# In-projection, retention, combination and RG-LRU of a hybrid decoder step run as one stage

## The reference, cut to what matters

```python
h = rmsnorm(x, norm_mix)                   # 1024 + 64 tokens, 1024 features
q, k, v, g, xl, yl = split(h @ w_in)       # 256, 256, 512, 512, 512, 512 columns
# retention, 4 heads, chunks of 128 tokens (samples: one chunk of 8 with their own state)
att = (q_c @ k_c.T) * decay
o   = att @ v_c + (q_c * q_dec) @ S
S   = S * c_dec + (k_c * k_dec).T @ v_c
ret = head_rms(o, ret_g) * silu(g)
# RG-LRU
x = causal_conv(xl)                        # 4 taps
r, i = sigmoid(x @ w_rg + b), sigmoid(x @ w_ig + b)   # 4 diagonal blocks of 128
a = exp(-8 r softplus(-lam));  b = sqrt(1 - a^2) * i * x
hl = scan(h_t = a_t h_{t-1} + b_t)
out = concat(ret, hl * gelu(yl)) @ w_out   # then residual, FFN, and layer 1
```

## Time and profile before

| | us |
|---|---|
| median of 3 runs | 3221.49 (3220.18 to 3224.18) |
| the profiled execution, its own time | 3216.29 |
| its span in the trace | 3214.6 |
| granted TensorE clock, mean | 0.95 |
| TensorE matmul / weight load busy | 2972.2 / 2810.3 |
| VectorE / ScalarE / GpSimd busy | 1359.8 / 757.0 / 183.7 |
| chain that ended last | TensorE 39%, DMA 2%, VectorE 2%, ScalarE 1% of the span |

### The profile page before, as it was taken

One profiled execution on the slowest core, in us unless ns is written; L12 is line 12 of the kernel. 1 busy time (PEld: TensorE's weight loads), 2 busy tenths in 40 slices (PEclk: granted clock), 3 DMA queues, 4 the chain that ended last, 5 costly groups with the idle time before them and its releaser, 6 DMA issues. The chain is left out here.

```text
span 3214.6 us, 47394 instructions
## 1 busy us (share of the span) xinstructions
PE 2972.2 (92%) x21277; PEld 2810.3 (87%) x21277; DVE 1359.8 (42%) x1651; ACT 757.0 (24%) x1082; POOL 183.7 (6%) x298
## 2 busy tenths in 40 slices
PE   6997852999999999999999799898899999999997
PEld 6997641999999999999999576666799999999997
DVE  4121248254343444445551255555543444443443
ACT  3100136131111111113221444444421111111110
POOL 0101110000000000002001111111000000000000
PEclk8998556999999999999999899999999999999999
DMA  5323110211111111112223766765301111111111
GB/s 180 110 82 122 51 56 21 84 40 53 40 40 40 53 40 42 51 53 97 82 82 96 271 212 198 249 206 172 134 28 48 45 40 53 50 43 40 40 40 56
DMA packets 130406, 276.23 MB, mean 86 GB/s; under 512 B 8737, under 2 KB 86773, under 8 KB 129696
## 3 DMA queue, kind: packets, MB, share of 16 engines
q1 hardware_dynamic: 107648, 184.83, 17.8%
q0 software_dynamic: 19136, 82.83, 7.5%
q10 hardware_dynamic: 3424, 5.57, 0.5%
HBM read 233.88 MB, written 39.33 MB: 85 GB/s over the span
## 5 line engine op out<-in xcount | busy, mean ns | idle before, releaser
L229 PE MATMUL psum<-h_hi,w_hi 128*128 128x364 f32 x2688 | 594.2, 330 | 18.2 <-DVE h_lo L355 7.2
L229 PE MATMUL psum<-h_hi,w_lo 128*128 128x364 f32 x2688 | 595.5, 330 | 0.0
L229 PE MATMUL psum<-h_lo,w_hi 128*128 128x364 f32 x2688 | 595.3, 329 | 0.0
L229 PEld LDWEIGHTS psum<-h_hi,w_hi 128*128 128x128 f32 x2688 | 468.1, 189 | 18.9 <-issue 13.3
L229 PEld LDWEIGHTS psum<-h_hi,w_lo 128*128 128x128 f32 x2688 | 469.2, 189 | 0.0
L229 PEld LDWEIGHTS psum<-h_lo,w_hi 128*128 128x128 f32 x2688 | 468.0, 189 | 0.0
L213 ACT ACTIVATE w_hi<-w_raw 128x2048 fp32r<-128x2048 f32 x96 | 183.7, 1914 | 830.8 <-PE psum L229 784.1
L1327 DVE TENSOR_TENSOR x_res<-x_res,psum 128x1092 f32<-128x1092 f32 x176 | 227.3, 1291 | 207.6 <-PE psum L229 207.6
L452 PE MATMUL psum<-w_hi,h_lo 128*128 128x256 f32 x992 | 278.7, 281 | 0.0
L452 PE MATMUL psum<-w_hi,h_hi 128*128 128x256 f32 x992 | 278.0, 280 | 0.0
L452 PE MATMUL psum<-w_lo,h_hi 128*128 128x256 f32 x992 | 277.9, 280 | 0.0
(11 more groups left out here) (313 smaller groups left out, 3169.2 us busy)
## 6 DMA issues: line engine op xcount, KB each, us to landing
cache_tile<-in_cache_k SPq DMA_DIRECT2D x64, 512.0 KB, 9.2
cache_tile<-in_cache_v SPq DMA_DIRECT2D x64, 512.0 KB, 3.7
w_raw<-in_w_ffn_gate SPq DMA_DIRECT2D x22, 1024.0 KB, 5.2
w_raw<-in_w_ffn_up SPq DMA_DIRECT2D x22, 1024.0 KB, 5.1
w_raw<-in_w_ffn_down SPq DMA_DIRECT2D x22, 1024.0 KB, 4.8
w_raw<-in_w_in_att SPq DMA_DIRECT2D x12, 1024.0 KB, 7.1
w_raw<-in_w_in_rec SPq DMA_DIRECT2D x10, 1024.0 KB, 5.2
park_x<-x_res POOLq DMA_DIRECT2D x2, 4368.0 KB, 15.4
```

The lines of the kernel that those rows point to most:

```text
L229: mm = pe.matmul(PS[:, bank + c, 0:CW], st[:, slot, wc:wc + P], mv[:, k, c * CW:(c + 1) * CW], start=(i < NCH), stop=(i >= 3 * NCH * nk - ...
```

## The change

Stages 2 to 5 and the output projection's stage become one. Nothing of the projections goes to DRAM any more, and the kernel has 4 meetings where it had 8.

- Stage 1: VectorE copies all 9 turned tiles. ScalarE squares x in its token-major form with a running sum as it arrives; the chain of 1/rms and the diagonal tile are made there, so the feature-major squares, their sums and the sums' matmuls of the first norm are gone. `split_lo(0)` and the vectors come in the middle.
- Order of the blocks: `COL = (6, 8, 7, 9, 0, 1, 2, 3, 4, 5)`, that is x, y, x, y, q, k as 12 feature-major tiles, then v and gate, 18 token-major units each. Tiles 0, 1, 4, 5 are x of the groups 0 to 3, tiles 2, 3, 6, 7 are y.
- RG-LRU: VectorE and ScalarE follow `D_ORDER` and `A_ORDER`, into which the tile evacuations ("ev"), the splits ("w") and the groups' steps are written. `GR`, `GI`, `AA`, `SA` and `YB` are single buffers. The gate matmuls of group j stand inside feature-major tile 2j+2 as three pairs, before the slices k = 2, 4 and 6, in banks 6 and 7; pair c waits until ScalarE has read pair c-1.
- Retention: q and k stay in SBUF; `first(c)` (turned keys, q times k) and `second(c)` (output, state) stand between the v units, `second(t-2)` after the even and `first(t-1)` after the odd unit of token tile t. The output is token-major (attention as the stationary operand), and the head norm is done on it at once by a small chain (`squares`, `inverse`, `root`, `scale`).
- Gate: 18 token-major units with silu in token-major form, each result turned by two transposes (`turn`) two units later and placed by ScalarE (`place`). The samples' retention lies between these units.
- Output projection: `high`/`low` split its operands as soon as the last gate unit has used the slices (`KO` order, LRU's first); its first tile follows slice by slice.
- Pool: X is parked after four small loads; the retention tables are loaded after the last LRU group; X comes back after the last turn.

The diff, cut to its core:

```diff
+        for f in range(2 * N_FM):
+            if f % 2 == 0:
+                pe.wait_ge(wl_done, f // 2 + 1)
+            if f >= 2:
+                pe.wait_ge(fm_out, f - 1)
+            fm_tile(pe, 3 * (f % 2), f // 2 % RING, col_tiles(f % 2), hook(f), HHI, HLO, fm_in)
...
+                if f in YF[0:1] + XF[2:3] + YF[2:3] + (8,) and k in (2, 4, 6):
+                    gates(f // 2 - 1, k // 2 - 1)
...
+        def gates(j, c):
+            if c == 0:
+                pe.wait_ge(l_d, dn["c2", j])
...
+            if 3 * j + c:
+                pe.wait_ge(g_out, 2 * (3 * j + c))
+            for bank, wt in ((6, WR), (7, WI)):
+                pe.matmul(PS[:, bank, 0:CW], wt[:, j, :], XC[j % 2][:, c * CW:(c + 1) * CW],
+                          start=True, stop=True).then_inc(g_in, 1)
...
+    D_ORDER += conv(0) + conv(1) + [("w", 3), ("ev", YF[0])] + scan(0) + [("gi", 0), ("g", 0), ("m", 0)]
+    D_ORDER += [("ev", YF[1]), ("gi", 1), ("g", 1), ("w", 4)] + conv(2) + scan(1) + [("m", 1)]
+    D_ORDER += conv(3) + [("w", 5), ("ev", YF[2]), ("gi", 2), ("g", 2)] + scan(2) + [("m", 2)]
+    D_ORDER += [("ev", YF[3]), ("gi", 3), ("g", 3), ("w", 6), ("ev", 8)] + scan(3) + [("m", 3)]
+    D_ORDER += [("ev", 9), ("w", 7), ("ro", 0), ("ev", 10), ("ev", 11), ("w", 8)]
+    A_ORDER = [("x", 0), ("x", 1), ("w", 3)] + [(x, 0) for x in ("ri", "e", "t", "a", "sq", "q", "gt")]
+    A_ORDER += [("q", 1), ("w", 4), ("gt", 1), ("ri", 1), ("e", 1), ("t", 1), ("x", 2), ("a", 1), ("sq", 1)]
+    A_ORDER += [("x", 3), ("w", 5)] + [(x, 2) for x in ("ri", "e", "t", "q", "gt", "a", "sq")]
+    A_ORDER += [("q", 3), ("w", 6), ("gt", 3)] + [(x, 3) for x in ("ri", "e", "t", "a", "sq")] + [("w", 7), ("w", 8)]
...
+            elif x == "ri":
+                act.wait_ge(l_sp, 6)
+                if j:
+                    act.wait_ge(l_d, dn["m", j - 1])
+                for c in range(NCH):
...
+        pe.wait_ge(l_out, 1)
+        for t in range(NT):
...
+            unit(2 * t, 6, t)
+            if t >= 2:
+                second(t - 2)
...
+            unit(2 * t + 1, 7, t)
+            if t >= 1:
+                first(t - 1)
...
+        for u, (b, t) in enumerate(GSEQ):
...
+            unit(2 * NT + u, 8 + b, t)
+            if u == 0:
+                second(NCHK - 1)
+                sample_first()
+            if u == 2:
+                sample_out()
+            if u == 3:
+                sample_state(0)
+            if u == 4:
+                sample_turn()
+            if u == 5:
+                sample_state(1)
+            if u >= 2:
+                turn(u - 2)
```

More of the change, by code:

```diff
@@ new lines, in prep_sums, with prep_spread @@
+    def prep_sums(pe, q):
+        prep_wait(pe, q, "sq_sum", KT - 1)
+        for t in range(NT):
+            mm = pe.matmul(PS[:, 7, 2 * t:2 * t + 2], sq_buffer(q, 0)[0][:, win(t):win(t) + P], ones[:, 0:2],
+                           start=True, stop=True)
+        mm.then_inc(prep_sem["sums"], 1)
+    def prep_spread(pe, q, parts):
+        prep_wait(pe, q, "diag", 1)
+        for bank, t0, m in parts:
+            if t0 == KT:
+                prep_wait(pe, q, "spread_out", 1)
+            for t in range(t0, t0 + m):
+                r0 = t * P - win(t)
+                mm = pe.matmul(PS[:, bank, (t - t0) * P:(t - t0 + 1) * P - r0], ones[:, :], DIA[:, t, r0:P],
+                               start=True, stop=True)
+            mm.then_inc(prep_sem["spread"], 1)
@@ L408, in prep_spread @@
[L408 to L434 removed]
+            if t == 5:
+                split_lo(dve, 0, 0)
+                dve.wait_ge(vt_done, 1)
+                dve.tensor_copy(vec[:, :], PS[:, 7, 0:NV])
@@ L570, in build, with tm_unit @@
+            if used is not None and i < KT - 1:
+                mm.then_inc(used, 1)
+        return mm
+    def tm_unit(pe, bank, slot, t, done, cols=None):
+        return tm_part(pe, bank, slot, t, range(KT), None, None, cols).then_inc(done, 1)
     stages = {e: [] for e in ("pe", "act", "dve", "pool")}
@@ L995, in s5_act, with tok_scale, rec_act @@
+    v3 = lambda t: t.rearrange("p (c w) -> p c w", c=NCH)
+    def tok_scale(t, half):
+        if t < QT:
+            return RHF[:, t:t + 1] if half else rtok[:, t, 0:1]
+        return RSM[:, 1:2] if half else RSM[:, 0:1]
+    def rec_act(act):
+        for k in range(KT):
+            prep_hi(act, q2, G_MIX[0], k)
+        spread_out(act, q2, SPREAD[:2])
+        split_hi(act, 1, 1, first=True)
+        spread_out(act, q2, SPREAD[2:])
+        split_hi(act, 2, 2, first=True)
         act.activation(SC[:, 0, :], vec[:, V_LAM:V_LAM + 4], ACT.Abs).then_inc(l_sp, 1)
@@ new lines, in rec_act @@
+        for u in range(NGU):
+            if u == NGU - 1:
+                high(0)
+            gate(u)
+            if u == 0:
+                squares(NCHK - 1)
+                act.wait_ge(s_kt, 1)
+                act.wait_ge(r_s, NCHK)
+                act.activation(KTS[:, :, :].rearrange("p h k -> p (h k)"), PS[0:NS, 0, 0:RH * DK],
+                               ACT.Copy).then_inc(s_kts, 1)
+                split_hi(act, 10, 10 % RING)
+            if u == 1:
+                root(NCHK - 1)
+            if u == 2:
+                act.wait_ge(s_o, 1)
+                for e in range(2):
+                    op = act.activation(OS[:, :, :].rearrange("p (g e) w -> p e g w", e=2)[:, e],
+                                        PS[:, (3, 0)[e], 0:2 * NS].rearrange("p (g w) -> p g w", g=2), ACT.Copy)
+                op.then_inc(s_os, 1)
+            if u == 4:
+                squares(QT)
+            if u == 5:
+                root(QT)
+            if u >= 2:
+                place(u - 2)
@@ L1047, in s5_dve, with rec_dve @@
+        for i in range(1, 4):
+            high(i)
+        place(NGU - 2)
+        place(NGU - 1)
+        for i in range(4, KT):
+            high(i)
+        split_hi(act, 11, 11 % RING)
+        split_hi(act, 12, 12 % RING)
+        act.wait_ge(s_ss, 64)
+    def rec_dve(dve):
+        for k in range(KT):
+            prep_low(dve, q2, G_MIX[0], k)
+        split_lo(dve, 1, 1)
+        split_lo(dve, 2, 2)
         dve.wait_ge(l_sp, 3)
@@ new lines, in rec_dve, with gate @@
+        dve.wait_ge(fm_out, 2 * N_FM)
+        for t in range(NT):
+            if t >= 2:
+                state(t - 2)
+                inverse(t - 2)
+            if t >= 1:
+                decay(t - 1)
+            if t >= 2:
+                scale(t - 2)
+            if t >= 1:
+                attend(t - 1)
+        split_lo(dve, 9, 9 % RING)
+        def gate(u):
+            b, t = GSEQ[u]
+            n = P if t < QT else NS
+            dve.wait_ge(tm_out, 2 * NT + u + 1)
+            dve.scalar_tensor_tensor(GG[u % 2][0:n, :], GT[u % 2][0:n, :], 1.0, GG[u % 2][0:n, :], ALU.add,
+                                     ALU.mult).then_inc(m_u, 1)
+            dve.wait_ge(m_u, u + 1)
+            dve.wait_ge(r_oo, t + 1)
+            dve.scalar_tensor_tensor(GT[u % 2][0:n, :], GG[u % 2][0:n, :], 0.5, ON[0:n, t, b * BW:(b + 1) * BW], ALU.mult,
+                                     ALU.mult).then_inc(m_in, 1)
@@ L1651, in cache_load @@
             if j == 0:
[L1652 removed]
+                sp.wait_ge(met, 4 * 2)
             if u == 8:
```

1339 lines of the change are left out of this document (670 added, 669 removed).

## The result

| | before | after |
|---|---|---|
| median, us | 3220.84 (3219.20 to 3224.18) | 3050.22 (3048.41 to 3056.48) |
| ratio | | 0.9472, 95% interval 0.9456 to 0.9489 |
| the profiled execution, its own time | 3216.29 | 3056.48 |
| its span | 3214.6 | 3054.7 |
| mean granted clock | 0.95 | 0.98 |

What follows compares the result with a forecast made beforehand. Bound before the output projection by a chain over VectorE, ScalarE, DMA and slow TensorE, behind it by TensorE's queue. Steps put the second evacuation at 417.7 against 593.4, -175.7: 3040.6 profiled, plus 5.2 gives median 3046; range 3018 to 3085.

Steps and rivals of the forecast that it cites:

- (a): Stage 1: VectorE copies nine tiles and makes the norm's chain and diagonal; +2.5 us, first matmul at 31.7.
- (b): Twelve feature-major tiles with gate matmuls: 24.7 us of new waits, 6.8 of low clock behind them, over at 229.4.
- (c): 18 v units with retention chunks between: 82.5 us, to 311.9, nothing waits, pace 10.0 us.
- prediction's own signs of being wrong: Pace in (c) not 10.0 us, waits in (b) far from 25 us, or any changed length behind the second evacuation.
- (d): 18 gate units, last chunk, samples' retention and turns: 81.8 us, to 393.7, with a 4.0 us wait at the samples' outputs.
- (e): Output projection: operand splits stay ahead, X's return costs nothing, second evacuation at 417.7 against 593.4, -175.7 us.
- the loop of `m`, `ri` and the pairs: RG-LRU: a group's second gate pair waits for `ri`, which from group 1 waits for the previous group's `m`.
- rival 2: LRU chain longer than walked: 1.4 us more per table switch or hand-over, some 14 us, 3060; chance 12%.
- Rival 1: Small float32 matmuls in (c) and (d) don't get faster at full clock: 36 us more, 3082; chance 10%.
- the condition for harm: Output projection: X's return, 13.9 us, would cost something only from 24 us on; 40 would cost 16.
- Rival 3: The LRU is hidden: waits in (b) vanish, 31.5 us go, 3014; chance 6%.
- Rival 4: TensorE's clock never rises in the new stage: +320 us, 3366 at worst, slower than before; chance 1%.

Runs made afterwards that it cites:

- e11_again: The changed kernel run and profiled once more, unchanged: median 3050.96 us, second evacuation of the output projection at 423.53.
- e1: Only ScalarE's order differs from the changed kernel, reading a group's gates (`ri`) first: gate waits 22.5 us against 22.7, second evacuation of the output projection 425.44.
- e2: VectorE's and ScalarE's LRU orders woven against the changed kernel, same operations: median 3024.81 us, ratio to before 0.9389.
- e3: Against the changed kernel, ScalarE takes the last chunk's norm root before block 10's high half: second evacuation of the output projection 420.87 against 426.25.
- e9: Against e8, samples' retention outputs turned round so the 128-column state moves and spread queries are stationary: median 3006.47 us, ratio to before 0.9341.
- e6: Against the changed kernel, X brought back three times in a row and VectorE waits for the third: third residual starts at 453.60 against 438.23.
- e5: Against the changed kernel, each retention chunk's `second` stands directly behind its `first`, no unit between: 3104.7 us, second evacuation of the output projection 475.09.
- e8: Against the changed kernel: woven LRU orders, gate matmuls one tile later, early root, last turn inside the output projection: median 3013.49 us, ratio to before 0.9365.
- e4: Against the changed kernel, the samples' four output heads stand behind four different gate units: second evacuation of the output projection 422.88 against 426.25.
- e10: Against the changed kernel, `second(t-2)` stands directly ahead of `first(t-1)`, small matmuls in one row: token tile 10.6 us, second evacuation of the output projection 429.78.
- e7: Against the changed kernel, last turn behind the output projection's first slice, first low half and first residual earlier: execution 3055.49 us, second evacuation 421.64.

## Why the prediction was right, point by point

The total came out, 4 us above the forecast, with three misses in the parts that moved the event, all of them of TensorE's clock or of small matmuls. That it came so close is in part luck. Steps (a) and (b) were 3.4 us too long and (c) 3.4 us too short. And the forecast put the median 5.2 us above the profiled execution, while it came 6.3 us below it: the profiled execution took 3056.48 where 3040.6 had been worked out, 8.5 us of it up to the event and 7.2 behind it. In e11_again the same kernel took 3046.56, 6.0 above. By the prediction's own signs of being wrong two were met: the pace in (c) was 10.6 and not 10.0, and the length behind the second evacuation changed in one execution (2628.4) and not in the other (2621.3), so this second one is not laid to the change.

No run undoes the joining of the stages as a whole. That the 280 us went is read from the two profiles; the runs test the orders, the clock and X's return inside the new stage.

| step | forecast | profile after |
|---|---|---|
| (a) first matmul | 31.7 | 30.42 |
| (b) tile 0 evacuated | 58 to 59 | 54.94 |
| (b) gate waits, four | 4.1, 4.9, 8.4, 7.3 | 2.6, 4.6, 8.2, 7.3 |
| (b) twelve tiles over | 229.4 | 226.0 |
| (c) pace of a token tile | 10.0 | 10.6 |
| (c) units and chunks over | 311.9 | 311.9 |
| (d) wait at the samples | 4.0 | 2.25 |
| (d) samples' outputs | 10 | 15.2 |
| (d) last turn, first slice | 1.7, 1.0 | 1.6, 0.9 |
| (e) first two tiles of the output projection | 24 | 26.9 |
| (e) first residual starts | about 407 | 421.84 |
| from the second evacuation to the end | 2621.2, unchanged | 2628.4 |

(a), (b). Walking the three written-out orders side by side gave the waits to within 0.3 us in three of four groups, and the event behind them within 3.4 us. What I called the cause (the loop of `m`, `ri` and the pairs) was confirmed by e1 and e2. In groups 1 to 3 moving ScalarE's `ri` alone gained nothing; group 0's wait was ScalarE's. The low clock behind a wait was 1.6 to 2.1 us each (group 1: 4.3 us from 104.00 to 108.30 for 2.3 us of work), I had charged 1.7. Table loads cost what their row says: in the profile after a load of 1.28 us at 67.56 stands between a split that ends at 67.55 and an operation at 68.86. The drain that the Trainium skill (ScalarE: Activation LUTs, What ACT_TABLE_LOAD costs) adds to each switch, for about 2.66 us in all, is not in this trace, and rival 2, which rested on such a delay, gave 14 us that did not come.

(c) Rival 1 fell: the small float32 matmuls are twice as fast at 1.00. An output block (eight matmuls) starts at 315.82 and the state behind it at 319.05, 3.23 us against the 5.76 of the earlier trace rows. I had 2.9 by halving, and nothing for the first matmul of each unit behind such a block, which takes 0.22 us instead of 0.12. That made the pace 10.6 instead of 10.0, 3.4 us in all (85.9 instead of 82.5), as much as (b) was early.

(d) The one term that was mis-sized by its mechanism. I halved the samples' outputs by the row of another form, which was nearly right for a block at 1.00 (1.95 us for 3.58), and took the clock for granted because TensorE would not wait in the row; the 1.7 us of low clock that I charged was for the wait. The miss is 5 us for the outputs and 2.6 for the unit behind. e3 shows that most of it does not need the wait: without it the outputs took 13.1 us (326.12 to 339.21) instead of 15.2, and the unit behind was slow all the same. e9, the same work with 128 columns moved, stays at 1.00.

(e) 2.8 us of low clock that no step had. It comes in some executions and not in others. The first residual was put 1 to 2 us behind tile 0 and came some 8 us behind it, since the walk had block 12 split after it and at 414, and it is split before it, at 419.63. It cost nothing, by 0.2 us in e11.

Together: -3.4 (a, b), +3.4 (c), +5.7 (d: 87.5 us from 311.9 to 399.4 instead of 81.8), +2.8 (e) make the +8.5 between 417.7 and 426.25.

X's return was harmless, as forecast, and the condition for harm was the one given, by e6; what came close to harm was the order on VectorE. Rival 3 (the LRU hidden) was not what the change does, but it is what e2 makes of it: 25 us of the 31.5 that I had priced it at. Rival 4 (the clock never rises) I held to be 1%, on the ground that dense work stands between the waits. That ground held for this kernel, but e5 shows how thin it is: with a wait of 2 us in each token tile the clock is at half for some 10 us of every 17, and the kernel loses 54 us (3104.7 against 3050.2).

## What to carry to other kernels

Work that is put between dense matmuls is worth more than the idle time that it fills, since TensorE's clock pays or charges for it as well: here 15 us of waits in eight pieces cost about 50. Put the dependent pieces of a chain so far apart that another unit covers every answer of the slower engines, and look at the order of the engine on which two such chains meet, before asking for buffers. A milestone read from one execution is good to a few us only; compare local durations behind an equal event.

## What the runs showed of the hardware

- A row of 8-column float32 matmuls without a gap was followed by a granted clock of 0.50 (e3: from 331 on, dense units up to 326.1 and no wait; e8: from 297 on, 2.2 us after the row began), and a single head of 2.2 us between dense units by about 3 us of 0.50 in the unit behind it (e4, from 343.9 to 347.2). A row of 128-column float32 matmuls of 4.8 us (e10) and of 9.0 us (e9) kept 1.00.
- At 1.00 eight 8-column matmuls with their 64x128 stationary operands took 1.95 us, and eight 128-column ones with 64x64 operands 1.96 us: the narrow form saved nothing even at full clock.
- 2 us of idle time next to 1 us of small matmuls was followed by 0.50 already at the first matmul behind it (e5, 269.93); in the first chunk of e5 a wait of 0.73 us inside the row was followed by 0.50 from 239.0 on, 2 us behind the wait; 1.6 and 1.0 us of idle time around a single turn were followed by 0.50 in seven executions and by 1.00 in two.
- From the second evacuation to the end the same code took 2621 to 2632 us (shortest before, in e4 and in e11, longest in e7). Up to tile 11, which came between 222.9 and 226.4, executions with the same code ahead of it differed by up to 3.5 us.
